# Identity products ahead of and behind the stages of a decoder step, and an output stage that rounds its second tile earlier

## What is computed

```
layer 0 mixer: gated short convolution beside sparse attention over the 256 best keys of an indexer, one output projection
layer 1 mixer: mLSTM matrix memory, chunk by chunk (c, n, m carried), output gate, one output projection
both layers:   cross attention over 256 memory rows, then square(relu(xn @ w1)) @ w2 with 4096 hidden columns
```

## Time and profile before

| | us |
|---|---|
| median of 3 runs | 3671.59 |
| lowest, highest | 3671.28, 3672.29 |
| profiled execution, its own time | 3671.36 |
| span of the profiled execution | 3669.5 |
| TensorE busy in it | 3246.2 (88%) |
| VectorE busy in it | 1803.8 (49%) |
| ScalarE busy in it | 1403.3 (38%) |
| mean granted clock of TensorE | 0.934 |

### The profile page before, as it was taken

How to read it: one execution, slowest core, us unless ns; L and a number is a source line. 1 busy time by engine, 2 the same in 40 slices (tenths; PEclk the granted TensorE clock), 3 DMA queues, 4 the chain that set the end, 5 groups by cost and what they waited for, 6 DMA issues and landing times. The chain is left out here.

```text
span 3669.5 us, 44268 instructions
## 1 busy us (share of the span) xinstructions
PE 3246.2 (88%) x17291; PEld 2584.5 (70%) x17291; DVE 1803.8 (49%) x3171; ACT 1403.3 (38%) x2389; POOL 152.6 (4%) x168
## 2 busy tenths in 40 slices
PE   8879994876978799999998998996888799999996
PEld 6724642444776699899886677674786699899885
DVE  5677998632335544444444431056335444444543
ACT  6452212632344433433444441153334333433443
POOL 0020110033000000000000000012000000000000
PEclk9989996997989899999999897997999899999998
DMA  3122122056031333343352210012020433333452
GB/s 103 25 66 81 42 74 78 1 181 221 24 99 57 121 130 123 115 134 119 127 161 81 64 35 24 23 25 80 23 104 30 144 123 130 115 128 125 127 161 105
DMA packets 226195, 341.90 MB, mean 93 GB/s; under 512 B 34375, under 2 KB 163119, under 8 KB 225988
## 3 DMA queue, kind: packets, MB, share of 16 engines
q1 hardware_dynamic: 214212, 297.13, 25.1%
q0 software_dynamic: 11776, 41.95, 3.5%
HBM read 328.56 MB, written 10.19 MB: 92 GB/s over the span
## 5 line engine op out<-in xcount | busy, mean ns | idle before, releaser
L638 DVE TENSOR_TENSOR s_mlp_w2l<-s_mlp_w2b,s_mlp_w2h 128x1024 fp32r<-128x1024 f32 x192 | 235.1, 1226 | 585.1 <-ACT s_mlp_w2h L524 585.1
L172 PE MATMUL ps<-s_mlp_xl,s_mlp_w1h 128*128 128x384 f32 (+1 forms) x1536 | 499.3, 325 | 9.0 <-DVE s_mlp_xl L656 9.0
L174 PE MATMUL ps<-s_mlp_xh,s_mlp_w1h 128*128 128x384 f32 (+1 forms) x1536 | 495.9, 323 | 0.0
L173 PE MATMUL ps<-s_mlp_xh,s_mlp_w1l 128*128 128x384 f32 (+1 forms) x1536 | 495.4, 323 | 0.0
L524 ACT CAST s_mlp_w2h<-s_mlp_w2b 128x1024 fp32r<-128x1024 f32 x192 | 201.5, 1050 | 588.8 <-PE ps L174 588.7
L172 PE MATMUL ps<-s_mlp_w2l,s_mlp_hh 128*128 128x512 f32 x1024 | 406.0, 396 | 20.5 <-DVE s_mlp_hl L675 16.2
L174 PE MATMUL ps<-s_mlp_w2h,s_mlp_hh 128*128 128x512 f32 x1024 | 403.1, 394 | 0.0
L173 PE MATMUL ps<-s_mlp_w2h,s_mlp_hl 128*128 128x512 f32 x1024 | 403.0, 394 | 0.0
L172 PEld LDWEIGHTS ps<-s_mlp_xl,s_mlp_w1h 128*128 128x128 f32 x1536 | 289.8, 189 | 41.1 <-issue 34.9
L173 PEld LDWEIGHTS ps<-s_mlp_xh,s_mlp_w1l 128*128 128x128 f32 x1536 | 289.8, 189 | 6.2
L174 PEld LDWEIGHTS ps<-s_mlp_xh,s_mlp_w1h 128*128 128x128 f32 x1536 | 289.6, 189 | 0.0
(11 more groups left out here) (559 smaller groups left out, 5589.0 us busy)
## 6 DMA issues: line engine op xcount, KB each, us to landing
s_mlp_w1b<-w_ff SPq DMA_DIRECT2D x96, 1024.0 KB, 6.2
s_mlp_w2b<-w_ff SPq DMA_DIRECT2D x96, 1024.0 KB, 8.4
x_kb<-cache_mem_k SPq DMA_DIRECT2D x16, 512.0 KB, 7.1
x_vb<-cache_mem_v SPq DMA_DIRECT2D x2, 4096.0 KB, 20.6
s_orows_raw<-w_in_odd SPq DMA_DIRECT2D x32, 256.0 KB, 3.0
s_convsel_w<-w_in_even SPq DMA_DIRECT2D x12, 512.0 KB, 3.9
x<-x_prompt SPq DMA_DIRECT2D x8, 512.0 KB, 5.6
ev_mixT<-w_in_even SPq DMA_DIRECT2D x16, 256.0 KB, 4.1
```

What stands on the lines that cost most here:

```text
L172: nc.tensor.matmul(out, ah, bl, start=first, stop=False, skip_group_check=True)
L173: nc.tensor.matmul(out, al, bh, start=False, stop=False, skip_group_check=True)
L174: return nc.tensor.matmul(out, ah, bh, start=False, stop=last, skip_group_check=True)
L638: nc.vector.tensor_tensor(w2l[:, s % RING], w2b[:, c % 3, s % FC, :], w2h.bitcast(F32)[:, s % RING], ALU.subtract).then_inc(low2, 1)
```

## The change

A helper issues n products of the identity with itself, 128 by 512 columns in fp32, into one bank:

```
+def keep_warm(nc, G, bank, n):
+    for _ in range(n):
+        nc.tensor.matmul(G.ps[:, bank, :].rearrange("p (a t) -> p a t", a=4), G.ident[:], bc(G.ident[:].unsqueeze(1), [P, 4, P]),
+                         start=True, stop=True)
```

It is called on TensorE at nine places of the code, 3 to 14 products each, 17 calls in a run. Those in `stage_out` and `stage_mlp` come once in each of the four output stages and in both MLPs, except for the 14:

```
 stage_out
                 pe.wait_ge(s_turned, 2)
+            keep_warm(nc, G, 2, 3)
             sample(0)
...
+            pe.wait_ge(added, NT - RING + 2)
+            keep_warm(nc, G, 2 * (NT % RING), 4)
 stage_mlp
+            keep_warm(nc, G, 7, 9)
             for e in range(6):
                 turn(e, e)
+            keep_warm(nc, G, 7, 4)
             up(0)
...
+            if name == "mlp0":
+                keep_warm(nc, G, bank(), 14)
 stage_conv_select, last
+            keep_warm(nc, G, 4, 4)
 stage_qk_gates, first
+            keep_warm(nc, G, 7, 7)
             pe.wait_ge(side_in, 64)
 stage_mlstm, first and last
+            keep_warm(nc, G, 7, 3)
             pe.wait_ge(made, 2)
...
+            pe.wait_ge(inter_kept, N)
+            keep_warm(nc, G, 3, 4)
```

In `stage_out` with `rows=True` the rounding of tile 1 moves ahead of the sample's tail, on ScalarE and on VectorE; the roundings of tiles 2 to 7 stay where they were:

```
 scalar
-            if not rows:
-                round_tile(1)
+            round_tile(1)
             tail_sample()
             for t in range(NT):
-                if rows and t + 1 < NT:
+                if rows and 1 <= t < NT - 1:
                     round_tile(t + 1)
 vector
-            if not rows:
-                rest_of_tile(1)
+            rest_of_tile(1)
...
             for t in range(NT):
-                if rows and t + 1 < NT:
+                if rows and 1 <= t < NT - 1:
                     rest_of_tile(t + 1)
```

## The result

| kernel | executions | median, us | lowest to highest | ratio to before, 95% interval |
|---|---|---|---|---|
| before | 14 | 3690.9 | 3669.84 to 3702.71 | |
| after | 14 | 3657.07 | 3645.74 to 3663.19 | 0.9922 [0.9901, 0.9942] |

The change makes the kernel faster by 0.8% (the ratio 0.9922; the quotient of the two medians is 0.9908), and its median lies 4.5 us above the forecast of 3652.6, inside the range. What nobody could read from three executions is the first row: eleven more executions of the same kernel before split into two groups, six of the 14 between 3669.8 and 3677.7 (median 3671.9) and eight between 3687.9 and 3702.7 (median 3698.5). The executions of after form no such groups. So the change does two things: it takes about 15 us off the lower group, and it does away with the upper one, which is 27 us longer. The prediction knew of the first alone.

A forecast was written before the change was run, and what follows sets the result against it. TensorE was taken as the bound inside nearly every stage, with idling and half clock at stage borders; 5.8 + 6.2 + 4.0 + 1.5 + 1.5 = 19.0 us off 3671.4, plus 0.2, gave 3652.6 us, range 3643 to 3663.

The forecast's parts named there:

- Sum: Whole kernel: the mLSTM, odd output, MLP, even output and gate terms together save 19.0 us.
- mLSTM start: Three products ahead of the first mLSTM unit keep full clock for units 0 and 1: 5.8 us saved.
- The base: Starting time of the sum: the profiled execution's 3671.4 us, 0.2 below the median of three runs.
- Odd output stage: Reorder lets tile 1 start without waiting; a new 4.1 us stall comes ahead of tile 2: net 6.2 us saved.
- Rival 4: Odd output stage: no new stall, 12.2 us saved in place of 6.2, total 3646 us; chance 0.06.
- MLP starts: Fills of nine, then four products bring the first multiplications to full clock: 2.0 us each, 4.0 saved.
- Even output and gates: Three products at the even output start save 1.5 us; seven ahead of the gate products save 1.5 us.
- All else at nothing: Products at stage ends, behind the first MLP and at cross-attention output starts, and the added waits, change nothing.
- (1): The clock is not held by the fills; only the reorder's gain stays, less late fills: 3666 us, chance 0.15.
- (2): The products themselves run at half clock, 1.74 us each, so fills end late: 18.6 us slower, 3690; chance 0.04.
- (3): Cross-attention output stages also stay at full clock, saving up to 3.0 us in each of two: 3646 us, chance 0.10.

The follow-up runs named there:

- again: The kernel of before, run again unchanged: median 3680.8 us, ratio 1.0009.
- again3: The kernel of before, run unchanged a third time for another trace: a single execution of 3695.83 us.
- tile2_early: mlp_fill7 with tile 2 of the odd output stage also rounded ahead of the sample rows' tail: 3649.65 us, ratio 0.9897.
- mlp_fill7: The whole change with the second fill of each MLP start lengthened from four products to seven: 3647.35 us, ratio 0.9913.
- trim_tile2: tile2_early without any identity products but those at the mLSTM start (3) and in the MLPs (9 and 7): 3653.24 us, ratio 0.9919.
- mlstm_reorder: Before with only the three products at the mLSTM start and the new order in the odd output stage: 3658.3 us, ratio 0.9916.
- again2: The kernel of before, run unchanged once more for a trace: a single execution of 3698.24 us.
- tile2_bank: tile2_early with TensorE's wait ahead of tile 2 replaced by one for VectorE's first sum of the sample rows: 3647.59 us, ratio 0.9903.
- fills_only: The whole change without the reorder, all identity products but the odd output stage in its old order: 3656.13 us, ratio 0.9929.

## Why the prediction came out right, point by point

- **Sum.** By the stage table, the five terms forecast at 19.0 us came to 18.9 in the profiled pair: mLSTM 6.9 (133.4 to 126.5), odd output 7.3 (127.9 to 120.6), even output 2.5, the MLP starts 1.2 and 1.0, gates 0. That the sum is so near is luck in part: three terms were 1.0 to 1.1 us too small each, two were 1.8 and 1.5 too large. The spans differ by 8.2 only, because other stages were longer in this execution of after: cross attention 0 by 3.6, sample attention, which has no edit, by 2.0, the output stage of cross attention 0 by 1.9 (67.6 to 69.5). Such differences appear between executions of one kernel too: sample attention took 140.8 us in *again* and 143.7 in *again3*. In cross attention 0 it goes with the clock (0.90 in after, 0.94 in before). Why they all went one way here is open.
- **mLSTM start: right mechanism, mis-sized.** 5.8 was forecast, at most 7 (half of both slow units). Against the lower group it was 6.9: unit 2 had still begun at half clock, and the fill did not end 0.5 us late but as the first operand arrived. Against the upper group it was 35.2 (161.7 to 126.5). "The later units keep full clock" was true of the one trace read, not of the kernel.
- **The base.** The step that failed is the last of the sum, "3671.4 - 19.0": it took the median of three executions for the time of the kernel. That the total still lies near the forecast is because the change removes exactly what those three did not show.
- **Odd output stage: right.** No gap ahead of tile 1; a stall ahead of tile 2 ended by VectorE's subtraction, 5.01 us for 4.1 (3.5 to 6.0 in the five traces with this order); half clock behind it, as taken. The stage gained 7.3 for 6.2. Rival 4 needed tile 2 rounded ahead of the samples; *tile2_early* did that and the stall did not go: the rival overlooked that the bank of the sample sums is tile 2's bank.
- **MLP starts: 2.2 of 4.0.** The term had its wait wrong. The fill was placed to end at 1238.9 ahead of a multiplication at 1240.04, 1.1 us short; it left 2.28 us idle. The first multiplication waits for VectorE's last subtraction, and that comes no sooner when the transposes run faster (6.7 us behind the third scaled tile before, 6.9 after). The last eight transposes and the first multiplication, before and after:

```profile
1233.40 1.97 PE L453 MATMUL ps<-ident,s_mlp_y 128*128 128x128 f32 x8 [0.78 <-ACT s_mlp_y L530]
1240.04 0.66 PE L172 MATMUL ps<-s_mlp_xl,s_mlp_w1h 128*128 128x384 f32 x1 [4.67 <-DVE s_mlp_xl L656]
...
1236.21 1.09 PE L461 MATMUL ps<-ident,s_mlp_y 128*128 128x128 f32 x8 [1.84 <-ACT s_mlp_y L542]
1243.02 0.41 PE L179 MATMUL ps<-s_mlp_xl,s_mlp_w1h 128*128 128x384 f32 x1 [2.29 <-DVE s_mlp_xl L668]
```

  The wait behind the transposes grew from 4.67 to 5.72 us. With the clock held, as in *mlp_fill7*, the two starts are worth 2.6 and 2.2 us (21.7 to 19.1, 21.2 to 19.0), a little more than the forecast.
- **Even output and gates.** The even output start gained 2.5 for 1.5 (1.9 between the means of all traces). The gate fill gained nothing for 1.5, its lower bound.
- **All else at nothing.** Not contradicted: *trim_tile2*, which also lacks the even output start and the gates, is 3.6 us slower in median, within what the courses of *attend* make.
- **Rivals.** (1) fell with the mLSTM stage, though it is right for the gates and for the MLP starts of this trace. (2) fell: eight entries of the second MLP fill take 3.60 us, 0.45 each, near the 0.435 forecast, and of the long first fill only a part of the first 3.87 of 9.50 us ran at half clock. (3) fell: in after the first cross-attention output stage still has half clock in its opening, and the stage takes 67.5 to 69.5 us in the six traces with products at its start, 67.6 to 69.3 in the eight without.

## What to carry to other kernels

Take more than one trace before counting on a base: a kernel whose clock can come back early or late has two times, and three executions may show one. Fill the idle stretch ahead of a stage in which TensorE alone sets the pace, and let the fill reach the first product: of six traced MLP starts with a fill that stopped some 2 us short four lost the clock, of eight with one that reached it none. The mean granted clock is no measure of time: the traced execution of *mlstm_reorder* took 3654.6 us at 0.938, that of the whole change 3663.2 at 0.948. Full clock that passes while TensorE runs fills or waits raises the mean and saves nothing; how much of the difference that is was not worked out.

## What the runs showed of the hardware

That the clock can stay at 1.2 GHz under dense work was not expected: in *again2* TensorE was busy for 61.73 of 62.14 us at half clock, behind two units at half clock as well, and then rose; in *before* the same instructions were at half clock for two units, 14.52 us, and the third unit took 5.7. The Trainium skill, TensorE: Matmul & The Clock Gate, section What's actually happening, has sustained work bring full clock; that trace does not agree.

The clock can also fall while TensorE is busy. In *tile2_bank* the 144 gate products begin at full clock and lose it 1.45 us later, without a pause; in after, behind seven products at full clock and 2.22 us idle, they had half clock for all of their 28.34 us.

```profile
2229.36:2230.81 1.45, 1.45 (x13) 1.00 0.94 335
2230.81:2256.45 25.64, 25.64 (x134) 0.50 0.01 4
```

One idle stretch can go either way. In after, 2.2 to 2.3 us were followed by half clock at the MLP start and at the gates, and 1.93 us at the second MLP (2869.05 to 2870.98; 0.62 over the next 4.49 us); in *fills_only* the same 1.93 us at the second MLP were not. The 2.30 us of the earlier trace rows, on which the prediction rests the half clock behind its new stall and its answer to rival 3, look like this in *again2*, the same program:

```profile
1530.23:1532.53 2.30, 0.00 (x1) 1.00 0.45 74
1532.53:1535.87 3.34, 3.34 (x15) 1.00 0.99 323
```

Six of the fourteen traces have full clock behind that stretch, eight do not. What decides between the courses, there, in *attend* or in the mLSTM stage, no run here shows.
